# An attention stage whose head groups are put one head after the other, with the projections beside the score units

## The chip, the core and the metric

The kernel runs on one core of a Trainium2 chip. Its time is the device time of that core in microseconds, from launch to end. Five engines work side by side, each with its own queue of instructions, in which everything is done in order: TensorE (PE, matrix products and transposes into PSUM, which has eight banks), VectorE (DVE), ScalarE (ACT), GpSimd (POOL) and SyncE (SP), which here only issues DMAs. They wait for each other by semaphores: a wait stands in front of an instruction and holds up everything behind it in the same queue.

## The reference

Two layers of a streaming encoder, on 1024 prompt frames and on 8 running streams of 16 frames. The first is a gated linear recurrence, the second multi-head latent attention. The change is in the attention of the prompt:

```python
cq = rms_norm(proj[..., :Q_LORA], q_norm_g)
q = einsum('btr,re->bte', cq, w_uq).reshape(bsz, t, B_HEADS, NOPE_DIM + ROPE_DIM)
q_rope = rope(q[..., NOPE_DIM:], pos)
# 16 heads; per head, blocks of 128 queries against all earlier keys (chunks of 64)
s = (q_nope . (c w_uk) + q_rope . kr) * (128 + 64) ** -0.5
p = softmax(where(key_chunk <= q_chunk, s, -1e30))
out = (p @ (c w_uv)) * silu(gate)
```

The queries of the 128 sample rows are only projected here (q_lat, q_rope) and used in the samples' attention, the next stage.

## The kernel before

The stages follow each other: recurrence (to about 550 us), output product and norms of layer one, input product of layer two (to about 1000), attention of the prompt head by head in pairs (to about 1667), attention of the samples (to about 1850), output product. Each fp32 product is made of three passes over a high and a low part: ScalarE rounds a value to the high part, VectorE subtracts for the low one, TensorE runs low*high, high*low, high*high (lines 118 to 120).

Attention works on pairs of heads, `body(pr, first, last)`, eight times (the middle six in a loop). A pair consists of two kinds of work.

*Projections*, in the order of `PROJ` (19 steps): QA0 to QA2 and QB0 to QB2 (queries of head A and B, three groups of 384 rows), R0 to R2 (the part of both heads' queries that is rotated), KA0, KA1, KB0, KB1 (keys), V0 to V3 (values), UT and QL (for the samples' queries). Each writes one bank; ScalarE and VectorE then read it, and `proj_out` says that it is free. The R steps are read by VectorE alone (`rope`, one multiplication of 128 partitions and four of 32), then GpSimd adds two halves, ScalarE rounds (the last group with a copy for the samples ahead of it) and VectorE makes the low part (`rope_low`). The scratch of the rotation lies in `p`, the tile of attention weights, so that the first weights (`exp(0)`) and the last rotation exclude each other.

*Score units*, 16 of them, u = 0 to 15, in the order of `ORDER`: a group is (head, 256 queries), a unit is 128 of its queries, and groups are taken two at a time with their units alternating (`unit`, `place_of`). A unit has between one and eight blocks of keys. Its steps: `scores` (TensorE into bank 0, 1 or both for even u, 2 or 3 or both for odd u; it waits until `exp` two units before has read them), `largest` (VectorE), `exp` (ScalarE), `inverted` (VectorE), the scaling by GpSimd, `turn` (TensorE, transposes through banks 4 to 6, rounded by ScalarE and VectorE in `turned`), and for each group `values` (TensorE, bank 7), `gated` (VectorE, the multiplication by the gate) and the store of the result.

All engines walk the same list, by hand: `scores` runs three units ahead of `turn`. Eleven projections (R0 to V0) come ahead of unit 0 and the next pair's QA0, QA1, QA2 and QB0 beside units 14 to 16. SP loads two gates ahead, stores each group's result, and at the beginning of the last pair issues the samples' first loads (`samples.load_first`).

## Time and profile before

| | us |
|---|---|
| median of 3 runs | 2052.42 (2051.8 to 2053.69) |
| the profiled execution | 2052.9 |
| its span, first to last instruction | 2051.1 |
| TensorE busy | 1936.9 (94%) |
| VectorE, ScalarE, GpSimd busy | 1116.0, 721.4, 467.5 |
| mean granted clock of TensorE | 0.984 |

"Busy" counts the time in which at least one instruction runs on the engine. For matmuls, which overlap, it says how long there was any, and their distance in time (from start to start) says what one costs. A row of the timeline with a bracket gives the idle time ahead of it and the instruction whose end released it. The granted clock is 1.00 at 2.4 GHz and 0.50 at 1.2.

### The profile page before, as it was taken

To read this page: it belongs to the slowest core of one execution; us is meant where nothing else is said; L and a number is where in the kernel's file an instruction comes from. 1 tells how busy PE (TensorE), PEld (TensorE's weight loads), DVE (VectorE), ACT (ScalarE), POOL (GpSimd) and SP (SyncE) were. 2 spreads that over 40 slices of the span, in tenths; PEclk is the share of its full clock that TensorE was granted. 3 is DMA by queue.
4 is the path that set the end of the run, shared out by engine and by line. 5 is a ranking of instruction groups with operands and counts; after the bars stand their busy time and mean duration, and the time that the engine had idled before them with its cause. 6 is when DMAs were issued, how large, how long until landed. Compare 5 with 4: busy or idle time off the path is not lost.

```text
span 2051.1 us, 31461 instructions
## 1 busy us (share of the span) xinstructions
PE 1936.9 (94%) x11755; PEld 1821.6 (89%) x11755; DVE 1116.0 (54%) x1964; ACT 721.4 (35%) x1247; POOL 467.5 (23%) x390
## 2 busy tenths in 40 slices
PE   7999999999869999999999999999899889999997
PEld 6999999999848899999989989888899779988886
DVE  3365545654657612332466676666666666763643
ACT  3333232323221132211254453543534447761100
POOL 0121222212211110000153352544433510000111
PEclk9999999999979999999999999999999989999999
DMA  5121122211164212232211110211111412364421
GB/s 163 42 75 45 41 73 65 64 32 53 35 228 138 88 44 76 76 101 76 85 56 51 42 50 23 65 49 32 55 50 41 128 55 68 94 226 139 139 92 41
DMA packets 190337, 158.78 MB, mean 77 GB/s; under 512 B 36176, under 2 KB 174928, under 8 KB 190000
## 3 DMA queue, kind: packets, MB, share of 16 engines
q1 hardware_dynamic: 184608, 137.31, 22.0%
q10 hardware_dynamic: 5184, 18.88, 2.6%
q0 software_dynamic: 464, 1.48, 0.2%
q8 instruction: 56, 0.92, 0.2%
q14 instruction: 25, 0.20, 0.0%
HBM read 115.78 MB, written 41.84 MB: 77 GB/s over the span
## 4 chain that ended last, share of the span: by engine, by line
PE 46%; issue 11%; DVE 5%; ACT 4%; POOL 3%; SPq 1%; DMA 1%; ACTq 0%; DVEq 0%; POOLq 0%
PE ps L118 14%; PE ps L120 13%; PE ps L119 13%; POOL h_p L1595 3%; PE ps L1699 1%; DVE h_mx L1894 1%; PE ps L1682 1%; PE ps L1681 1%; ACT h_p L1793 1%; DVE s_mx L2448 1%; DMA m_w_raw<-in_w_out_a 1%; SPq L2067 1%; DVE h_pt_l L112 1%; PE ps L2157 0%; ACT h_w_h L107 0%
## 5 line engine op out<-in xcount | busy, mean ns | idle before, releaser
L118 PE MATMUL a_pj<-act_h,a_w_l 128*128 128x384 f32 x768 | 276.8, 360 | 7.5 <-DVE act_l L112 7.5
L1600 POOL TENSOR_SCALAR h_p<-h_p,h_rsum 128x128 f32<-128x128 f32 (+7 forms) x128 | 220.4, 1728 | 220.9 <-DVE h_rsum L1898 220.2
L119 PE MATMUL a_pj<-act_l,a_w_h 128*128 128x384 f32 x768 | 261.2, 340 | 0.0
L120 PE MATMUL a_pj<-act_h,a_w_h 128*128 128x384 f32 x768 | 260.8, 340 | 0.0
L118 PE MATMUL ps<-act_h,m_c_l 128*128 128x384 f32 x480 | 163.7, 341 | 4.1 <-DVE act_l L112 2.4
L120 PE MATMUL ps<-act_h,m_c_h 128*128 128x384 f32 x480 | 163.3, 340 | 0.0
L119 PE MATMUL ps<-act_l,m_c_h 128*128 128x384 f32 x480 | 163.1, 340 | 0.0
L118 PEld LDWEIGHTS a_pj<-act_h,a_w_l 128*128 128x128 f32 x768 | 145.3, 189 | 12.8 <-DVE act_l L112 8.2
L119 PEld LDWEIGHTS a_pj<-act_l,a_w_h 128*128 128x128 f32 x768 | 145.6, 190 | 3.4 <-issue 3.4
L120 PEld LDWEIGHTS a_pj<-act_h,a_w_h 128*128 128x128 f32 x768 | 145.2, 189 | 0.0
L107 ACT ACTIVATE h_pt_h<-ps 128x128 fp32r<-128x128 f32 (+2 forms) x192 | 87.0, 489 | 114.6 <-PE ps L1699 113.5
L1793 ACT ACTIVATE h_p<-ps,h_mx 128x128 f32<-128x128 f32 (+7 forms) x128 | 95.0, 742 | 85.5 <-DVE h_mx L1894 81.1
L118 PE MATMUL ps<-o_w,o_g 128*128 128x512 f32 x288 | 112.1, 389 | 0.0
L119 PE MATMUL ps<-o_w,o_g 128*128 128x512 f32 x288 | 112.0, 389 | 0.0
L120 PE MATMUL ps<-o_w,o_g 128*128 128x512 f32 x288 | 112.0, 389 | 0.0
L112 DVE TENSOR_TENSOR h_pt_l<-ps,h_pt_h 128x128 fp32r<-128x128 f32 (+2 forms) x192 | 100.2, 550 | 19.1 <-ACT h_pt_h L107 18.9
L118 PE MATMUL ps<-h_pt_h,h_v_l 128*128 128x256 f32 x320 | 93.4, 292 | 15.9 <-DVE h_gate L1912 15.9
L1595 POOL TENSOR_TENSOR h_p<-h_p 64x384 f32<-64x384 f32 x48 | 58.4, 1217 | 208.0 <-DVE h_p L1853 206.6
L1894 DVE TENSOR_REDUCE h_mx<-ps 128x1 f32<-128x128 f32 (+7 forms) x128 | 97.0, 758 | 4.4
L118 PE MATMUL ps<-cq_h,h_w_l 128*128 128x384 f32 x288 | 97.7, 339 | 1.4 <-ACT h_pt_l L1811 1.4
L118 PE MATMUL ps<-h_kt_h,h_qn_l 128*128 128x384 f32 (+4 forms) x192 | 75.2, 391 | 23.9 <-ACT h_p L1793 16.4
L120 PE MATMUL ps<-cq_h,h_w_h 128*128 128x384 f32 x288 | 96.4, 335 | 0.0
(325 smaller groups left out, 4978.4 us busy)
## 6 DMA issues: line engine op xcount, KB each, us to landing
a_w_raw<-in_w_in_a SPq DMA_DIRECT2D x32, 512.0 KB, 4.1
m_c_raw<-in_w_in_b SPq DMA_DIRECT2D x20, 512.0 KB, 4.1
scratch_gate<-m_sg SPq DMA_DIRECT2D x16, 576.0 KB, 5.1
h_gate<-scratch_gate SPq DMA_DIRECT2D x64, 128.0 KB, 2.0
scratch_og<-h_gate SPq DMA_DIRECT2D x64, 128.0 KB, 1.7
o_w_raw<-in_w_out_b SPq DMA_DIRECT2D x16, 512.0 KB, 6.9
o_g_raw<-scratch_og SPq DMA_DIRECT2D x24, 256.0 KB, 4.1
a_factors<-in_x SPq DMA_DIRECT2D x9, 512.0 KB, 5.3
```

What stands on the lines that cost most here:

```text
L107: return nc.scalar.activation(high, x, ACT.Identity)
L112: return nc.vector.tensor_tensor(low, x, high.bitcast(F32), ALU.subtract)
L118: nc.tensor.matmul(out, ll, rh, start=first, stop=False)
L119: nc.tensor.matmul(out, lh, rl, start=False, stop=False)
L120: return nc.tensor.matmul(out, lh, rh, start=False, stop=last)
L1595: done = nc.gpsimd.tensor_tensor(rope_sums(tg)[:, e], rope_part(tg, 0)[rows], rope_part(tg, 1)[rows], ALU.add)
L1600: nc.gpsimd.tensor_scalar(weights_of(u), weights_of(u), rsum[:, u % PB], None, ALU.mult).then_inc(S["p_ready"], 1)
L1681: nc.tensor.matmul(out, rq[:, e, q], k.kr_l[:, kc], start=False, stop=False)
L1682: mm = nc.tensor.matmul(out, rq[:, e, q], k.kr_h[:, kc], start=False, stop=True)
L1699: mm = nc.tensor.transpose(bank[:, 4 + i % TB, j * P:j * P + P], p[:, u % PB, key * P:(key + 1) * P], k.ident[:])
L1793: nc.scalar.activation(weights_of(u), scores_of(u), ACT.Exp, bias=mx[:, u % PB], accum_out=rsum[:, u % PB]).then_inc(S["exp_done"], 1)
L1894: nc.vector.tensor_reduce(mx[:, u % PB], scores_of(u), AX.X if n <= BANK else AX.XY, ALU.max, negate=True).then_inc(S["max_done"], 1)
```

## The change

The groups are taken head by head: all four of head A, then all four of head B, a small one (at most four blocks of keys) together with a large one. As the even units are now the small ones, they need only bank 0, and bank 1 is free for one projection at a time. So the second head's projections and the sample step QL stand beside units 0 to 7 (`BESIDE`), the next pair's QA0, QA1, KA0, KA1 and QA2 beside units 9 to 13, and R0, R1, R2 around the last two value products. Ahead of unit 0 only V0 remains, ahead of unit 1 V1, UT, V2 and V3. `exp(0)` waits for the last rotated group. The weights of the next pair are split in units 6 to 8, two pieces each, instead of one piece in each of units 5 to 10. ScalarE does `exp(u + 3)` ahead of `turned(u)` instead of behind it. SP stores the sample queries after group 2 and issues the samples' loads, in the last pair, after group 4; ScalarE and VectorE take the first sample queries in unit 13 instead of 8.

```diff
@@ -1399,7 +1399,7 @@
-ORDER = [(0, 0), (1, 3), (0, 1), (1, 2), (1, 1), (0, 2), (1, 0), (0, 3)]
+ORDER = [(0, 0), (0, 2), (0, 1), (0, 3), (1, 0), (1, 2), (1, 1), (1, 3)]
...
-PROJ = ["QA0", "QA1", "QA2", "QB0", "R0", "R1", "R2", "QB1", "QB2", "UT", "KA0", "KA1", "KB0", "KB1",
-        "V0", "V1", "QL", "V2", "V3"]
-
-READS = ["QA0", "QA1", "QA2", "QB0", "R0", "QB1", "R1", "QB2", "UT", "KA0", "R2", "KA1", "KB0", "KB1",
-         "V0", "V1", "QL", "V2", "V3"]
-PROJ_BANK = [i % 8 for i in range(12)] + [4, 5, 6, 7, 4, 5, 6]
+PROJ = ["QA0", "QA1", "KA0", "KA1", "QA2", "R0", "R1", "R2", "V0", "V1", "UT", "V2", "V3",
+        "KB0", "QB0", "KB1", "QB1", "QB2", "QL"]
 NP = len(PROJ)
+PLACE = {"R1": 0, "R2": 2, "V0": 3, "V1": 4, "V2": 5, "V3": 6}
+FIRST_PLACE = {"QA0": 0, "KA0": 2, "KA1": 3, "QA2": 4, "R0": 5}
 HIGH_COUNT = {s: sum(x[0] != "R" for x in PROJ[:i + 1]) for i, s in enumerate(PROJ)}
...
-EARLY = {14: ["QA0"], 15: ["QA1"], 16: ["QA2", "QB0"]}
-NE = 4
+BESIDE = {0: ("KB0", 0), 1: ("QB0", 0), 2: ("KB1", 0), 3: ("QB1", 0), 5: ("QB2", 0), 7: ("QL", 0),
+          9: ("QA0", 1), 10: ("QA1", 1), 11: ("KA0", 1), 12: ("KA1", 1), 13: ("QA2", 1)}
+NE = 5
+
+
+def place(s, first):
+
+    return FIRST_PLACE[s] if first and s in FIRST_PLACE else PLACE.get(s, 1)
+
 PIECES = [2 * QD] * 4 + [2 * GQ] * 2
...
-            sp.wait_ge(S["proj_out"], pr * NP + NP)
-            sp.dma_start(d["scratch_ql"][bass.ds(pr, 1)].rearrange("o p t -> p (o t)"), flat(qlat[:])).then_inc(S["ql_stored"], 16)
-            sp.dma_start(d["scratch_qr"][bass.ds(pr, 1)].rearrange("o p t -> p (o t)"), flat(qr[0:RD])).then_inc(S["qr_stored"], 16)
-            if last:
-
-                sp.wait_ge(S["ql_stored"], 16 * PAIRS)
-                sp.wait_ge(S["qr_stored"], 16 * PAIRS)
-                k.samples.load_first(sp)
-            else:
+            if not last:
                 load_w(sp, pr + 1, False)
             for g in range(NG):
...
                     load_gate(pr, g + 2, False)
+                if g == 2:
+                    sp.wait_ge(S["proj_out"], pr * NP + NP)
+                    sp.dma_start(d["scratch_ql"][bass.ds(pr, 1)].rearrange("o p t -> p (o t)"), flat(qlat[:])).then_inc(S["ql_stored"], 16)
+                    sp.dma_start(d["scratch_qr"][bass.ds(pr, 1)].rearrange("o p t -> p (o t)"), flat(qr[0:RD])).then_inc(S["qr_stored"], 16)
+                if g == 4 and last:
+
+                    sp.wait_ge(S["ql_stored"], 16 * PAIRS)
+                    sp.wait_ge(S["qr_stored"], 16 * PAIRS)
+                    k.samples.load_first(sp)
         pairs(sp, body)
...
                 nc.gpsimd.tensor_scalar(weights_of(u), weights_of(u), rsum[:, u % PB], None, ALU.mult).then_inc(S["p_ready"], 1)
-                if last and u == 2:
+                if last and u == 10:
                     pool.wait_ge(S["proj_out"], PAIRS * NP)
                     k.samples.zero_first(pool)
+            if not last:
+                rope_adds(pr + 1)
         pairs(pool, body)
...
         def proj(pr, s, first):
-            i, b = STEP[s], PROJ_BANK[STEP[s]]
-            earlier = [j for j in range(i) if PROJ_BANK[j] == b]
+            i, b = STEP[s], place(s, first)
+            earlier = [j for j in range(i) if place(PROJ[j], first) == b]
             if s == "QA0":
                 pe.wait_ge(S["wl_ready"], pr * WPARTS + 4)
-            if s == "UT":
+            if s == "KA0":
                 pe.wait_ge(S["wl_ready"], pr * WPARTS + WPARTS)
             if earlier:
                 pe.wait_ge(S["proj_out"], pr * NP + earlier[-1] + 1)
             elif first:
                 k.bank_free(pe, b)
+            elif b == 1:
+                pe.wait_ge(S["proj_out"], pr * NP)
+            elif b < 4:
+
+                pe.wait_ge(S["exp_done"], pr * UNITS - 1 + b // 2)
             else:
-
-                if b < 4:
-                    pe.wait_ge(S["exp_done"], pr * UNITS - 1 + b // 2)
...
-
-                pe.wait_ge(S["proj_out"], pr * NP + STEP[("KA1", "KB1")[u]] + 1)
-                pe.wait_ge(S["rq_out"], pr * 3 + (1, 3)[u])
+                pe.wait_ge(S["proj_out"], pr * NP + STEP[("R1", "V0")[u]] + 1)
             else:
                 pe.wait_ge(S["exp_done"], pr * UNITS + u - 1)
+            if u in (0, 1, 5):
+
+                pe.wait_ge(S["rq_out"], pr * 3 + (1, 2, 3)[min(u, 2)])
+            if u in (8, 9, 13):
+
...
             proj(0, s, True)
         pe.wait_ge(S["zeroed"], 4)
         def body(pr, first, last):
-            for s in PROJ[NE:]:
-                if s in ("V1", "QL"):
-                    scores(pr, ("V1", "QL").index(s))
+            proj(pr, "V0", first)
+            scores(pr, 0)
+            for s in ("V1", "UT", "V2", "V3"):
                 proj(pr, s, first)
+            scores(pr, 1)
             scores(pr, 2)
             for u in range(UNITS):
+                if u in BESIDE and not (last and BESIDE[u][1]):
+                    s, n = BESIDE[u]
+                    proj(pr + n, s, first and not n)
                 if u + 3 < UNITS:
                     scores(pr, u + 3)
                 if u >= 4 and u % 4 < 2:
-                    values(pr, u // 4 * 2 - 2 + u % 2)
-                if u in EARLY and not last:
-                    for s in EARLY[u]:
-                        proj(pr + 1, s, False)
+                    values(pr, u // 4 * 2 - 2 + u % 2, first)
+                if u == UNITS - 1 and not last:
+                    proj(pr + 1, "R0", False)
                 turn(pr, u)
-            values(pr, NG - 2)
+            values(pr, NG - 2, first)
             if not last:
-                for s in EARLY[UNITS]:
-                    proj(pr + 1, s, False)
+                proj(pr + 1, "R1", False)
             else:
                 k.samples.turn_first(pe)
-            values(pr, NG - 1)
+            values(pr, NG - 1, first)
+            if not last:
+                proj(pr + 1, "R2", False)
...
         def exp(pr, u):
             act.wait_ge(S["max_done"], pr * UNITS + u + 1)
+            if u == 0:
+
+                act.wait_ge(S["rq_out"], pr * 3 + 3)
             if u >= PB:
...
         def body(pr, first, last):
-            for s in READS[NE:]:
-                if s == "V1":
-                    exp(pr, 0)
-                if s == "QL":
-                    exp(pr, 1)
+            proj(pr, "V0", first)
+            exp(pr, 0)
+            for s in ("V1", "UT", "V2", "V3"):
                 proj(pr, s, first)
+            exp(pr, 1)
             exp(pr, 2)
             for u in range(UNITS):
-                if u in EARLY and not last:
-                    for s in EARLY[u]:
-                        proj(pr + 1, s, False)
-                turned(pr, u)
+                if u in BESIDE and not (last and BESIDE[u][1]):
+                    s, n = BESIDE[u]
+                    proj(pr + n, s, first and not n)
                 if u + 3 < UNITS:
                     exp(pr, u + 3)
-                if 5 <= u < 5 + WPARTS and not last:
-                    split_high(act, pr + 1, u - 5)
-                if last and u == 8:
+                turned(pr, u)
+                if 6 <= u < 9 and not last:
+                    split_high(act, pr + 1, 2 * (u - 6))
+                    split_high(act, pr + 1, 2 * (u - 6) + 1)
+                if last and u == 13:
                     k.samples.first_queries_high(act)
             if not last:
-                for s in EARLY[UNITS]:
+                for s in ("R0", "R1", "R2"):
                     proj(pr + 1, s, False)
             else:
                 k.samples.first_keys_high(act)
...
         dve.wait_ge(S["table_loaded"], 32)
+        rope(0, 0, True)
+        rope(0, 1, True)
+
+        def ropes_end(pr, first):
+            rope_low(pr, 0)
+
+            dve.wait_ge(S["rq_out"], pr * 3 + 1)
+            rope(pr, 2, first)
+            rope_low(pr, 1)
+            rope_low(pr, 2)
+
+        ropes_end(0, True)
         def body(pr, first, last):
-            rope(pr, 0)
-            rope(pr, 1)
-            rope_low(pr, 0)
-
-            dve.wait_ge(S["rq_out"], pr * 3 + 1)
-            rope(pr, 2)
-            for s in READS[NE + 1:]:
-                if s[0] == "R":
-                    rope_low(pr, int(s[1]))
-                    continue
-                if s == "V1":
-                    largest(pr, 0)
-                if s == "QL":
-                    inverted(pr, 0)
-                    largest(pr, 1)
-                proj(pr, s)
+            proj(pr, "V0", first)
+            largest(pr, 0)
+            for s in ("V1", "UT", "V2", "V3"):
+                proj(pr, s, first)
+            inverted(pr, 0)
+            largest(pr, 1)
             inverted(pr, 1)
             largest(pr, 2)
             for u in range(UNITS):
                 if u + 2 < UNITS:
                     inverted(pr, u + 2)
+                if u in BESIDE and not (last and BESIDE[u][1]):
+                    s, n = BESIDE[u]
+                    proj(pr + n, s, first and not n)
                 if u + 3 < UNITS:
                     largest(pr, u + 3)
                 if u >= 4 and u % 4 < 2:
                     gated(pr, u // 4 * 2 - 2 + u % 2)
-                if u in EARLY and not last:
-                    for s in EARLY[u]:
-                        proj(pr + 1, s)
                 turned(pr, u)
-                if 5 <= u < 5 + WPARTS and not last:
-                    split_low(dve, pr + 1, u - 5)
-                if last and u == 8:
+                if 6 <= u < 9 and not last:
+                    split_low(dve, pr + 1, 2 * (u - 6))
+                    split_low(dve, pr + 1, 2 * (u - 6) + 1)
+                if last and u == 13:
                     k.samples.first_queries_low(dve)
             gated(pr, NG - 2)
             if not last:
-                for s in EARLY[UNITS]:
-                    proj(pr + 1, s)
+                rope(pr + 1, 0, False)
             else:
                 k.samples.first_keys_low(dve)
             gated(pr, NG - 1)
+            if not last:
+                rope(pr + 1, 1, False)
+                ropes_end(pr + 1, False)
```

VectorE, from one pair to the next. Before, in the new pair; h_p with h_cos and h_sin is `rope`, h_rq is `rope_low`, h_qn_l, h_kt_l and h_v_l are low parts of the queries of one head, keys and values, MEMSET and h_mx are `largest`:

```order
L1851 TENSOR_TENSOR h_p<-ps,h_cos 128x384
L1853 TENSOR_TENSOR h_p<-ps,h_sin 32x384 x4
...
L1866 SCALAR_TENSOR_TENSOR h_qn_l<-ps,h_qn_h 128x384
L1866 SCALAR_TENSOR_TENSOR h_rq<-h_p,h_rq 64x2x384
...
L1866 SCALAR_TENSOR_TENSOR h_qn_l<-ps,h_qn_h 128x384
...
L112 TENSOR_TENSOR h_kt_l<-ps,h_kt_h 128x512
L1866 SCALAR_TENSOR_TENSOR h_rq<-h_p,h_rq 64x2x384
...
L112 TENSOR_TENSOR h_kt_l<-ps,h_kt_h 128x512
...
L112 TENSOR_TENSOR h_v_l<-ps,h_v_h 128x512
...
L1890 MEMSET ps 64x64
L1894 TENSOR_REDUCE h_mx<-ps 128x1
```

After, from the last gate multiplication of a pair (h_gate) on:

```order
L1937 TENSOR_TENSOR h_gate<-ps,h_gate 128x256
L1876 TENSOR_TENSOR h_p<-ps,h_cos 128x384
L1878 TENSOR_TENSOR h_p<-ps,h_sin 32x384 x4
L1891 SCALAR_TENSOR_TENSOR h_rq<-h_p,h_rq 64x2x384
L1876 TENSOR_TENSOR h_p<-ps,h_cos 128x384
L1878 TENSOR_TENSOR h_p<-ps,h_sin 32x384 x4
L1891 SCALAR_TENSOR_TENSOR h_rq<-h_p,h_rq 64x2x384 x2
...
L112 TENSOR_TENSOR h_v_l<-ps,h_v_h 128x512
...
L1915 MEMSET ps 64x64
L1919 TENSOR_REDUCE h_mx<-ps 128x1
```

Between the last `rope` and the first `largest` stood two query parts, four key parts and one value part; now only the value part stands there, and the last gate multiplication of the pair before stands ahead of rope(1).

SP in the last pair. Before (scratch_og is the store of a group, h_gate the load of a gate, s_ql, s_qr, s_kr, s_c and in_cache_ckv the samples' loads):

```order
L1569 DMA scratch_ql<-h_qlat 128x512
L1570 DMA scratch_qr<-h_qr 64x256
L2071 DMA s_ql_raw<-scratch_ql 128x8x512
L2072 DMA s_qr_raw<-scratch_qr 64x8x256
L2063 DMA h_w_raw<-in_cache_ckv 128x8x256
...
L2067 DMA s_kr_raw<-out_krope_sample 16x64
L1581 DMA scratch_og<-h_gate 128x256
L1562 DMA h_gate<-scratch_gate 128x256
L1581 DMA scratch_og<-h_gate 128x256
L1562 DMA h_gate<-scratch_gate 128x256
```

After:

```order
L1578 DMA scratch_og<-h_gate 128x256
L1567 DMA h_gate<-scratch_gate 128x256
L2103 DMA s_ql_raw<-scratch_ql 128x8x512
L2104 DMA s_qr_raw<-scratch_qr 64x8x256
L2095 DMA h_w_raw<-in_cache_ckv 128x8x256
...
L2099 DMA s_kr_raw<-out_krope_sample 16x64
L1578 DMA scratch_og<-h_gate 128x256
L1567 DMA h_gate<-scratch_gate 128x256
L1578 DMA scratch_og<-h_gate 128x256 x2
```

The samples' loads moved behind the stores of five groups and the load of the seventh gate; the eighth gate's load stands behind them.

## Rows read from the trace of the kernel before

**Rows 1.** The page, part 1: busy us, share of the span, instructions.

```profile
PE 1936.9 (94%) x11755; PEld 1821.6 (89%) x11755; DVE 1116.0 (54%) x1964; ACT 721.4 (35%) x1247; POOL 467.5 (23%) x390
```

**Rows 2.** One head pair: us, busy (instructions), clock, DMA share, GB/s.

```profile
1191.00:1273.20 82.20, 77.09 (x504) 1.00 0.15 45
```

**Rows 3.** Waits of TensorE in 1000 to 1600: total us, times, longest us.

```profile
PE ps L118 <- ACT h_p L1793: 15.1, 21, 1.2
...
PE ps L118 <- DVE h_gate L1912: 9.9, 14, 1.0
...
PE ps L118 <- DVE h_kt_l L112: 6.8, 7, 1.0
...
PE ps L1699 <- POOL h_p L1600: 2.8, 7, 0.4
...
PE ps L1699 <- DVE h_pt_l L112: 1.3, 6, 0.2
```

**Rows 4.** Timeline, TensorE, start of a pair: start, us, [idle before <-releaser].

```profile
1287.60 0.41 PE L118 MATMUL ps<-h_kt_h,h_qn_l 128*128 128x320 f32 x1 [0.38 <-ACT h_p L1793]
```

**Rows 5.** Timeline, TensorE: first and thirteenth matmul of a row, 384 and 256 columns.

```profile
1257.05 0.33 PE L118 MATMUL ps<-cq_h,h_w_l 128*128 128x384 f32 x1
...
1259.13 0.33 PE L118 MATMUL ps<-cq_h,h_w_l 128*128 128x384 f32 x1
...
1192.32 0.28 PE L118 MATMUL ps<-h_w_h,ct_l 128*128 128x256 f32 x1
...
1193.76 0.37 PE L118 MATMUL ps<-h_kt_h,h_qn_l 128*128 128x448 f32 x1
```

**Rows 6.** Timeline, VectorE, start of a pair: rope(1), rope_low(0), the last rope_low.

```profile
1260.31 0.56 DVE L1851 TENSOR_TENSOR h_p<-ps,h_cos 128x384 f32<-128x384 f32 x1 [0.23 <-DVE h_p L1853]
...
1263.29 1.75 DVE L1866 SCALAR_TENSOR_TENSOR h_rq<-h_p,h_rq 64x768 fp32r<-64x768 f32 x1 [0.15 <-DVE h_p L1853]
...
1272.07 0.95 DVE L1866 SCALAR_TENSOR_TENSOR h_rq<-h_p,h_rq 64x768 fp32r<-64x768 f32 x1 [0.98 <-ACT h_rq L1767]
```

**Rows 7.** Timeline, GpSimd: the rotation's last two adds.

```profile
1268.07 2.71 POOL L1595 TENSOR_TENSOR h_p<-h_p 64x384 f32<-64x384 f32 x2 [2.16 <-DVE h_p L1853]
```

**Rows 8.** Timeline, ScalarE: copy and rounding of the last group.

```profile
1270.88 0.41 ACT L1766 COPY h_qr<-h_p 64x256 f32<-64x256 f32 x1 [2.60 <-POOL h_p L1595]
...
1271.19 0.84 ACT L1767 ACTIVATE h_rq<-h_p 64x768 fp32r<-64x768 f32 x1
```

**Rows 9.** Timeline: V's two roundings, largest and exp of five key blocks.

```profile
1274.85 0.68 DVE L112 TENSOR_TENSOR h_v_l<-ps,h_v_h 128x512 fp32r<-128x512 f32 x1
...
1276.37 0.59 ACT L107 ACTIVATE h_v_h<-ps 128x512 fp32r<-128x512 f32 x1
...
1289.73 0.82 DVE L1894 TENSOR_REDUCE h_mx<-ps 128x1 f32<-128x640 f32 x1
...
1619.21 0.80 ACT L1793 ACTIVATE h_p<-ps,h_mx 128x640 f32<-128x640 f32 x1 [0.62 <-DVE h_mx L1894]
```

**Rows 10.** Timeline, SP queue, last pair: first load, last key load, next store.

```profile
1614.37 0.39 SPq L2071 DMA_DIRECT2D s_ql_raw<-scratch_ql  x1
...
1627.38 2.28 SPq L2067 DMA_DIRECT2D s_kr_raw<-out_krope_sample  x1
...
1635.81 0.42 SPq L1581 DMA_DIRECT2D scratch_og<-h_gate  x1
```

**Rows 11.** Timeline, TensorE, last pair: values(3).

```profile
1641.10 0.55 PE L118 MATMUL ps<-h_pt_h,h_v_l 128*128 128x256 f32 x1 [5.55 <-DVE h_gate L1912]
```

**Rows 12.** Stretches with slow clock: us, busy (instructions), granted clock, DMA share, GB/s.

```profile
720.00:725.00 5.00, 4.75 (x19) 0.67 0.07 14
...
1642.00:1650.00 8.00, 8.00 (x45) 0.70 0.25 79
```

**Rows 13.** DMA issues: KB each, median us to landing.

```profile
s_qr_raw<-scratch_qr SPq DMA_DIRECT2D x1, 512.0 KB, 12.2
```

**Rows 14.** Timeline, TensorE, in the stage before attention.

```profile
720.25 0.44 PE L118 MATMUL ps<-act_h,m_c_l 128*128 128x384 f32 x1 [2.37 <-DVE act_l L112]
```

42 lines of the change are left out of this document (23 added, 19 removed).

## The prediction

> **What bounds the kernel now.** I read the page first: TensorE is busy 1936.9 of 2051.1 us [rows 1], so time goes either into its matmuls, which the change leaves as they are in kind and number, or into its waits. Then a table by stretches. One head pair lasts 82.2 us, of which TensorE is busy 77.1 at full clock [rows 2]; the reader is to see that 5.1 us a pair, 41 us over eight pairs, is all that any new order of the attention stage can win. Then the waits, summed over the first seven pairs [rows 3]. The largest are 15.1 us for the exponential (21 times, three a pair), 9.9 us for the gate multiply (14 times), 6.8 us for the second head's keys (once a pair, at the first score unit), and 2.8 and 1.3 us for scaled or turned weights just behind it. One of a pair's three waits for the exponential, 0.38 us, lies in the first units as well [rows 4]. So some 2.0 us (1.0 + 0.4 + 0.38 + 0.2) belong to the start of a pair, and 3.1 us to its middle, where a unit has nothing beside it.
>
> **What the change moves.** The names R0 to R2, V0 to V3, UT are the projection steps; s0, s1, ... the score units, exp, largest and turn what follows each of them. Before, behind a pair's last value product TensorE had R0, R1, R2, QB1, QB2, UT, KA0, KA1, KB0, KB1 and V0 to do before s0. They hid the rotation of the queries, a chain through four engines. After, R0 and R1 come a little earlier (before the last transposes and before the last values), but behind the last value product only R2, V0, s0, V1, UT, V2 and V3 are left before s1. Everything else lies beside units.
>
> *Start of a pair.* I call the end of the last value product 0. Twelve matmuls of 384 columns take 2.08 us and twelve of 256 take 1.44 [rows 5]. By that TensorE is through with R2 at 2.1 and with V0 at 3.55. On VectorE the last gate multiply ends at about 0.5, and only then come rope(1), rope_low(0), rope(2), rope_low(1) and rope_low(2). The same chain stands in the trace: rope(1) starts at 1260.31, rope_low(0) at 1263.29 and takes 1.75, and the last rope_low starts at 1272.07 and takes 0.95 [rows 6]. In between lie GpSimd's two adds for the last group, 2.71 us [rows 7], and ScalarE's copy and rounding, 1270.88 to 1272.03 [rows 8]. From start to end that is 12.7 us. Nothing of this is shorter in the new order, since its links wait for each other and not for TensorE; R2 is there in time, at 2.1. So rope_low(0) ends at 0.5 + 2.98 + 1.75 = 5.2 and the last rope_low at 13.1 to 13.2. V0's low part stands behind it in VectorE's queue, and takes 0.68 [rows 9]: 13.8.
> - s0 waits for rope_low(0) and for rope(1), whose bank it takes: 5.35 against 3.55, a wait of 1.8.
> - s0 (0.6), V1, UT (0.45), V2, V3 (three of 1.44) end at 10.75. s1 takes the banks of R2 and V0, so it waits for V0's low part: 13.85, a wait of 3.1.
> - s1 (ten matmuls of 320 columns), s2 and KB0 take 1.5 + 0.6 + 1.4 and end at 17.4. s3 waits for exp(1). Behind V0's low part come largest(0) 0.45, exp(0) 0.55, four roundings on ScalarE of some 0.5 (V1, UT, V2, V3; a row says 0.59, with starts closer than that), V3's low part 0.7, and largest(1) and exp(1) at 0.82 + 0.25 and 0.80 + 0.19 [rows 9]: 13.8 + 6.0 = 19.8. A wait of 2.3 to 2.4.
> - QB0 takes KB0's bank: KB0's two roundings follow exp(2), and TensorE waits about 0.7.
>
> Together 7.9 us against 2.0. There are eight such starts (the first has the same chain behind QA2, with R0 to R2 in a row): 5.9 x 8 = **+47**. Below, if the links overlap better, I put 3 a start, above 7.
>
> *Middle of a pair.* From unit 3 each unit has 1.4 to 2.1 us of projection beside it, and small and large units alternate. The waits for the exponential and for the gate are 0.5 to 1.2 us each; a projection in front covers each of them. Units 4, 6 and 8 have none (or QL's 1.05 in 7), but the widths there are mixed and I find no late exponential. What goes is 3.1 a pair in the first seven; the last pair has no next projections in its second half and gains nearly nothing: 3.1 x 7 = **-22**. It can't be more; at least zero.
>
> *A new wait for weights.* The six pieces of the next pair's weights are split in units 6 to 8, two a unit, and QA0 now needs four of them in unit 9. VectorE has some 9.2 us to do in units 6 to 8: three maxima 2.6, turned weights 2.1, six pieces 3.6 (some 0.6 each, near V's low part in size), a gate and reciprocals 0.9. TensorE has 8.1: three score units 3.9, QL and values(2) 2.5, turns 1.7. VectorE enters unit 6 about as late as it leaves it, with 1.4 us of chain behind TensorE's last score, so the fourth piece is out 1.7 us after TensorE asks for QA0, in the 7 pairs that have one, **+12**, between 0 and 20.
>
> *The last pair.* Before, the samples' first loads are issued at its start (1614.37), and the SP queue is free for the next store only at 1635.81: 21.4 us, for the queue is full [rows 10]. The gate of group 2 waits behind them, and TensorE stands 5.55 us [rows 11]; afterwards its clock is granted at 0.70 in 1642 to 1650 [rows 12], a mean between 2.4 GHz and 1.2, that is 2.4 us of work lost there. After, the same loads come behind the gate load for group 6, when gated(4) is done. I count from the end of s15: gated(4) at 2.0, its store landed and the gate load issued at 4.5. So the loads start at X = 4.5. The rotary queries land 12.2 us after issue [rows 13], which is at X + 12.6 = 17.1; ScalarE and VectorE wait for them in unit 13, in front of the transposed weights of units 14 and 15. The two split the queries in 1.0 and 1.2 us, values(6) starts at 20.2 instead of about 7.5, and the first keys' last load, issued 13.0 behind X [rows 10], lands at about 22.8. The sample transposes (3.3) and values(7) (2.9), in part at half clock, end at about 31. In the trace of before the last value product ends 13.8 behind s15. That is 17 more, less the 5.55 and the slow clock behind it (7.4 together, taken down by the usual wait of 0.9 and a little more at half clock): **+10**, between -7 (the loads are no hindrance) and +19.
>
> **Sum.** 47 - 22 + 12 + 10 = +47. The profiled execution took 2052.9 us around its span of 2051.1; the median of the three runs, 2052.42, is 0.5 below it. 2052.9 + 47 = 2100.
>
> **Rivals.**
> - *The clock falls at each start of a pair.* Where TensorE had waited 2.37 us, the next 5 us were granted 0.67 [rows 12, 14]: two thirds of them at 1.2 GHz, 1.65 us lost. Now a wait of 3.1 and one of 2.3 stand 3.5 us apart. What is slow between them is hidden by the second wait, what comes behind it is not: 1.65 x 8 = +13, so 2113, at most double. Against it: waits up to 1.2 left the clock at 1.00 [rows 2]. The Trainium skill (TensorE: Matmul & The Clock Gate, Part 1, HAM oscillation) says that gaps in the supply of matmuls put the array back to half rate and that it comes back only with sustained work; by that page this change, which gathers idle time in one place instead of spreading it, would pay the clock too, which is this rival and no part of my sum.
> - *The start is covered.* TensorE has 6.8 us of work between R2 and s1. If V0's low part were out at 8.9 instead of 13.8, s1 would not wait, and from 7 on neither s3. Then the work would hide the chain as eight projections did before, each start would stay at 2.0, and only the middle would count: 2052.9 - 22 + 10 = 2041, faster. For it: three of the V steps and UT are free of the chain. Against it: the 12.7 us of rows 6, which include no wait for TensorE.
> - *The last pair costs nothing*, since the queue takes the loads faster beside less other traffic: 47 - 22 + 12 - 7 = +30, 2083.
>
> **Chances.** Forecast 0.50, clock 0.20, last pair free 0.15, start covered 0.12, a mixture near no change 0.03. Range: the likeliest case's own is 2080 to 2120 (starts at 4.5 to 7 us, weights 0 to 20, end -7 to +19, not all at one side); toward the cheap starts it goes to 3 x 8 - 22 + 6 + 5 = +13, 2066, and with the clock to 2130. A measurement of this kernel can tell 0.2% (4 us) from no change. Faster 0.12, within 0.2% 0.04, slower 0.84.
>
> **What would show it.** In the profile after, seven times in the steady stage: TensorE waits of 1 to 3 us at the first, second and fourth score unit, released by VectorE (the rotated queries' low part, V's low part) and ScalarE (exponential); no waits of the gate multiply at TensorE; a wait for the split weights at QA0; a pair of about 87 us instead of 82.2. In the last pair, a wait of ScalarE of some 10 us at the samples' queries with TensorE standing behind it, and none at the gate of group 2. Wrong, if the second score unit waits under 1 us, or if the pair's period is below 82.

## The result, and the profile after

| | before | after |
|---|---|---|
| median of 4 runs, us | 2052.11 (2050.2 to 2053.69) | 2112.32 (2109.76 to 2113.41) |
| ratio, 95% interval | | 1.0292 [1.0274, 1.031] |
| span of the profiled execution | 2051.1 | 2108.0 |
| mean granted clock | 0.984 | 0.970 |

The kernel is 60 us slower. The page of after, part 1, beside [rows 1]: TensorE's share is smaller, and yet it is busy 18 us longer with the same 11755 instructions.

```profile
PE 1954.9 (93%) x11755; PEld 1841.2 (87%) x11755; DVE 1120.1 (53%) x1964; ACT 717.7 (34%) x1247; POOL 467.2 (22%) x390
```

TensorE's waits of after from 1000 to 1640 us (us in total, times, longest), against [rows 3]. The waits for the gate are gone, as are nearly all of those for the exponential. In their place stand V's low part, the split weights and the rotated queries, each once a pair, and one single wait of 11.3 us.

```profile
PE ps L118 <- DVE h_v_l L112: 18.8, 6, 3.2
PE ps L118 <- DVE h_w_l L112: 15.7, 7, 2.3
PE ps L118 <- DVE h_rq L1891: 11.4, 7, 1.7
PE ps L118 <- ACT h_pt_l L1836: 11.3, 1, 11.3
PE ps L118 <- DVE h_kt_l L112: 6.5, 12, 0.6
PE ps L118 <- ACT h_p L1818: 3.2, 4, 1.9
```

The waits of one steady pair, from the timeline of after (start, duration, line, idle time ahead and its releaser). They are those of s0, s1, s3 and QB0, against the 2.0 us before a pair's first units in [rows 3, 4], and at the end that of QA0:

```profile
1195.09 0.39 PE L118 MATMUL ps<-h_kt_h,h_qn_l 128*128 128x256 f32 x1 [1.62 <-DVE h_rq L1891]
1203.86 0.41 PE L118 MATMUL ps<-h_kt_h,h_qn_l 128*128 128x320 f32 x1 [3.17 <-DVE h_v_l L112]
1209.54 0.44 PE L118 MATMUL ps<-h_kt_h,h_qn_l 128*128 128x384 f32 x1 [0.44 <-ACT h_p L1818]
1212.13 0.45 PE L118 MATMUL ps<-cq_h,h_w_l 128*128 128x384 f32 x1 [0.45 <-DVE h_kt_l L112]
1242.24 0.44 PE L118 MATMUL ps<-cq_h,h_w_l 128*128 128x384 f32 x1 [2.26 <-DVE h_w_l L112]
```

The windows of after (us, busy of each engine, clock, DMA share, GB/s): a whole pair, then 4 us behind the wait of an s1, then 4 us around the wait of a QA0. The pair is 6 us longer than in [rows 2], 2.6 of them busy time, and in it the clock is low just behind the two longest waits.

```profile
1278.00:1366.20 88.20, 79.67 (x505) 74.93 (x504) 54.97 (x118) 36.32 (x84) 34.71 (x23) 0.96 0.14 42
1293.00:1297.00 4.00, 4.00 (x18) 3.51 (x16) 2.98 (x6) 2.09 (x7) 0.60 (x1) 0.60 0.00 1
1330.00:1334.00 4.00, 3.42 (x13) 3.43 (x14) 2.84 (x8) 2.19 (x5) 0.93 (x1) 0.66 0.10 33
```

The clock does not fall each time. In the fifth of the eight pairs (1366.7 to 1455.0 us) it stays at 1.00 behind the same wait of 3.17 us ahead of s1. There s3 waits 1.86 us instead of 0.44, and the pair is as long as its neighbours. In the second and the sixth pair it stays at 1.00 behind the same wait ahead of QA0, and these two pairs are 1.6 to 1.7 us shorter. The wait of s3 in the fifth pair with the window behind its s1, and the wait of QA0 in the sixth with the window behind it:

```profile
1386.25 0.44 PE L118 MATMUL ps<-h_kt_h,h_qn_l 128*128 128x384 f32 x1 [1.86 <-ACT h_p L1818]
1381.00:1385.00 4.00, 3.39 (x20) 2.72 (x19) 2.71 (x6) 2.40 (x6) 0.49 (x1) 1.00 0.02 7
1507.23 0.43 PE L118 MATMUL ps<-cq_h,h_w_l 128*128 128x384 f32 x1 [2.27 <-DVE h_w_l L112]
1508.00:1512.00 4.00, 4.00 (x30) 4.00 (x29) 2.84 (x9) 2.58 (x6) 0.70 (x2) 1.00 0.18 59
```

So in this kernel a slow clock behind s1 costs nothing, since s3 waits for ScalarE's exponential in any case, and one behind QA0 costs its full length. Why it falls in one pair and not in another, no run shows.

Where the 60 us are, from the ends of each pair's last value product. Before, pairs follow each other in 82.24 us. After, in 86.6, 88.4, 88.3, 88.3, 86.8 and 88.4: the six pairs in the middle cost 33.4 more. 4.9 us of projections moved from each pair into the one before it. With these counted to the pair that they belong to, the first pair costs 11.5 more and the last 15.8: 60.7 together. In the profiled execution the work ahead of the attention happened to be 3.7 us shorter, which makes the spans differ by 56.9. That part isn't touched by the change: in fourteen profiled kernels the first query projection starts anywhere from 994.2 to 1000.5 us, so below I compare pairs and not spans.

### The profile page after: what moved, and what is told of

Same layout as the page of the kernel before. It is cut to its first block, busy times and chain, and to the rows that moved or that the text cites. A ratio compares the mean times of both kernels' runs of the same rounds, so it can differ in the third digit from the quotient of the medians.

```text
span 2108.0 us, 31531 instructions
## 1 busy us (share of the span) xinstructions
PE 1954.9 (93%) x11755; PEld 1841.2 (87%) x11755; DVE 1120.1 (53%) x1964; ACT 717.7 (34%) x1247; POOL 467.2 (22%) x390
## 4 chain that ended last, share of the span: by engine, by line
PE 46%; issue 9%; DVE 8%; ACT 4%; POOL 3%; DMA 1%; ACTq 0%; SPq 0%; DVEq 0%; POOLq 0%
PE ps L118 14%; PE ps L119 14%; PE ps L120 14%; POOL h_p L1601 2%; DVE h_mx L1919 2%; PE ps L1714 1%; ACT h_pt_h L107 1%; DVE h_pt_l L112 1%; POOL h_p L1610 1%; ACT h_p L1818 1%; PE ps L1697 1%; PE ps L1696 1%; DMA s_qr_raw<-scratch_qr 1%; DVE s_mx L2480 1%; DMA m_w_raw<-in_w_out_a 1%
## 5 line engine op out<-in xcount | busy, mean ns | idle before, releaser
L118 PE MATMUL ps<-cq_h,h_w_l 128*128 128x384 f32 x288 | 103.6, 360 | 18.5 <-DVE h_w_l L112 15.7
L118 PE MATMUL ps<-h_kt_h,h_qn_l 128*128 128x256 f32 (+2 forms) x192 | 72.8, 379 | 37.4 <-DVE h_v_l L112 21.8
L119 PE MATMUL ps<-cq_l,h_w_h 128*128 128x384 f32 x288 | 99.3, 345 | 0.0
```

The lines of the kernel that those rows point to most:

```text
L118: nc.tensor.matmul(out, ll, rh, start=first, stop=False)
L119: nc.tensor.matmul(out, lh, rl, start=False, stop=False)
```

## The experiments

Unless said otherwise an experiment is the changed kernel with one edit. Ratios are to the kernel before, beside it on the same chip; after stands at 1.0292.

**Order of groups alone.** The kernel before, with one line changed.

```diff
-ORDER = [(0, 0), (1, 3), (0, 1), (1, 2), (1, 1), (0, 2), (1, 0), (0, 3)]
+ORDER = [(0, 0), (0, 2), (0, 1), (0, 3), (1, 0), (1, 2), (1, 1), (1, 3)]
```

> The kernel before with one thing of the change alone: the groups head by head, small with large, in place of the mixed order; the projections stay where they were. It asks what the order of groups does by itself. Theory (the waits in the middle of a pair come from units that have no projection beside them, and the start is covered by eight projections): a pair stays within 1 us of 82.2, the middle waits between 2 and 5 us, total within 0.5% of 2052. Rival (a good part of the loss comes from the new order, since the second unit has five blocks instead of seven and units are otherwise in balance): the pair grows by 3 us or more, or shrinks by 2 or more if the better balance is what wins the middle.

Measured 2059.2, ratio 1.0036 [1.0027, 1.0046]. A pair takes 83.4 us, 1.2 more than before. The order of the groups by itself is thus a small part of the 60 us; the rest comes with the other edits, the places of the projections, of the weights' pieces and of the samples' loads.

**The four zero blocks.** In the first pair TensorE stands 11.26 us ahead of V0:

```profile
1021.56 0.58 PE L118 MATMUL ps<-h_w_h,ct_l 128*128 128x256 f32 x1 [11.26 <-ACT h_pt_l L1836]
```

ScalarE's rows there show why. The four small blocks (L1836) stand in its queue behind the rounding of R2, and so behind the whole rotation:

```profile
1019.56 0.40 ACT L1788 COPY h_qr<-h_p 64x256 f32<-64x256 f32 x1 [3.90 <-POOL h_p L1601]
1019.88 0.84 ACT L1789 ACTIVATE h_rq<-h_p 64x768 fp32r<-64x768 f32 x1
1020.62 0.49 ACT L1836 ACTIVATE h_pt_h<-ident 128x128 fp32r<-128x128 f32 x2
1021.02 0.49 ACT L1836 ACTIVATE h_pt_l<-ident 128x128 fp32r<-128x128 f32 x2
```

```diff
-        for s in PROJ[:NE] + ["R0", "R1", "R2"]:
+        for s in PROJ[:NE]:
             proj(0, s, True)
         for x in (pt_h[0], pt_h[1], pt_l[0], pt_l[1]):
             nc.scalar.activation(x[:, 0, 0:P], k.ident[:], ACT.Identity, scale=0.0)...
+        for s in ("R0", "R1", "R2"):
+            proj(0, s, True)
```

> The changed kernel, but in the first pair ScalarE writes the four zero blocks (128 columns of the turned weights) ahead of R0, R1, R2 and not behind them. TensorE waits for these zeros before V0 of the first pair; in the changed kernel that wait was 11.26 us and ended with the zeros. Theory (the zeros stand in ScalarE's queue behind the rotation of the third group, so that V0, s0, V1, UT, V2 and V3 cannot lie beside the chain): the wait goes, and in its place come the waits of any other pair, 1.6 us at s0 and 3.1 us at s1; the 6.8 us of work between them move under the chain, and the granted clock stays at 1.00 in 1012 to 1028. Gain 6 to 9 us, 2112 becomes 2104. Rival (the chain of the first pair takes this long by itself and bounds whatever stands before it): no gain over 2 us, the wait is found again at s0 or s1 at its full size.

Measured 2109.04, 1.0274 [1.0256, 1.0292]. The wait is gone, and the trace has in its place waits like those of every other start (1.62 and 3.17 there):

```profile
1019.71 0.35 PE L118 MATMUL ps<-h_kt_h,h_qn_l 128*128 128x256 f32 x1 [2.36 <-DVE h_rq L1893]
1028.15 0.41 PE L118 MATMUL ps<-h_kt_h,h_qn_l 128*128 128x320 f32 x1 [2.88 <-DVE h_v_l L112]
```

The first pair is 6.3 us shorter. The ratio shows 4 us, and the intervals overlap, so the size rests on the trace.

**Weights one unit earlier.**

```diff
-                if 6 <= u < 9 and not last:
-                    split_high(act, pr + 1, 2 * (u - 6))
+                if 5 <= u < 8 and not last:
+                    split_high(act, pr + 1, 2 * (u - 5))
...
```

(and the same for the other piece and for the low parts on VectorE)

> The changed kernel, but the next pair's six weight pieces are split in units 5, 6 and 7 instead of 6, 7 and 8, two a unit as before. In the changed kernel TensorE waits 2.26 us for the fourth piece at QA0, seven times (15.7 us), and the 8 us behind it were granted 0.70 and 0.88 in part. Theory (VectorE and ScalarE reach the pieces too late for unit 9): the wait goes in every pair, 2.3 us plus up to 1.7 us of slow clock each, 7 times: gain 14 to 25 us, a pair 84.5 to 86 us instead of 88.4. Rival 1 (VectorE's backlog in units 5 to 8 bounds and only moves): TensorE waits as long elsewhere in units 7 to 10, gain under 5 us. Rival 2 (the pieces wait for QB2 at unit 5 and hold up the queue): slower.

Measured 2103.14, 1.0247 [1.023, 1.0264]: 9 us gained, not 14 to 25. QA0 no longer waits, but the fourth value product now does, 1.4 us for the gate, since the pieces stand ahead of that multiplication in VectorE's queue. The window of a pair tells the clock's share: its busy time fell by 1.3 us, and the clock around QA0 is 1.00.

```profile
1192.40:1278.80 86.40, 78.37 (x505) 73.69 (x505) 54.92 (x118) 36.23 (x84) 34.75 (x23) 0.98 0.15 43
1328.00:1332.00 4.00, 4.00 (x29) 4.00 (x28) 2.85 (x8) 2.58 (x6) 1.89 (x1) 1.00 0.00 0
```

So the wait of 2.26 had cost 3.6 with the slow clock behind it, and 1.7 came back at the gate and at a score unit. All six middle pairs take 86.3 to 86.5 us now. In two of them the clock stays at 1.00 behind s1 and s3 waits 1.87 us: no shorter.

**V3 computed three times.** This fills TensorE's idle time ahead of s1 with the same product again.

```diff
-                for j in range(2):
+                for j in [0, 1] * (3 if s == "V3" else 1):
```

> The changed kernel, but TensorE computes V3 three times over (24 more matmuls of 256 columns, 2.9 us, overwriting the same bank with the same values) just ahead of s1, where it waits 3.1 us for V0's low part. Nothing depends on the extra work. It asks what the slow clock behind that wait (0.60 in the 4 us from s1 on) costs. Theory A (the slow clock is hidden, because s3 must wait for exp(1) in any case: the wait at s3 is only 0.44 us because s1, s2 and KB0 ran slowly): the granted clock stays 1.00 there, the wait at s3 grows from 0.44 to 1.5 to 2.3 us, and the time changes by less than 4 us. Theory B (the clock costs 1.65 us at each start of a pair, 8 times): 8 to 14 us faster in spite of more work. Rival C (V3 comes later by the extra work and its roundings delay largest(1) and exp(1)): slower by 2 to 3 us a pair, 16 to 24 us.

Measured 2120.41, 1.0327 [1.0304, 1.0351], whose interval just touches that of after. The wait at s1 shrinks to 0.28, and that at s3 grows from 0.44 to 1.89:

```profile
1300.20 0.41 PE L118 MATMUL ps<-h_kt_h,h_qn_l 128*128 128x320 f32 x1 [0.28 <-DVE h_v_l L112]
1305.88 0.44 PE L118 MATMUL ps<-h_kt_h,h_qn_l 128*128 128x384 f32 x1 [1.89 <-ACT h_p L1818]
```

s3 starts 19.6 us behind the start of the pair in both kernels, so exp(1) did not come later by the added work. At full clock s2 and KB0 are done 1.45 us earlier, and TensorE waits that long for exp(1) instead. In two of the six middle pairs that wait has a low clock behind it. The two windows are of such a pair, behind s1 and behind s3, the second where after had full clock:

```profile
1300.00:1304.00 4.00, 3.79 (x21) 3.17 (x21) 2.58 (x8) 2.41 (x6) 0.00 (x0) 1.00 0.14 48
1306.00:1310.00 4.00, 4.00 (x15) 3.90 (x16) 2.10 (x7) 1.05 (x3) 2.78 (x2) 0.57 0.00 0
```

In after the stretch from 1298 us on, behind its s3, has full clock. Four of the six middle pairs last 88.2 to 88.4 us, as most of after's do: 2.9 us of products went into the idle time and the full clock behind s1 brought nothing. The two pairs with a slow stretch behind s3 last 89.2. And here the clock fell behind QA0 in all six, where after has two pairs without that. These two things make the 5.0 us by which the six are longer; 1.9 more are in the first pair, where TensorE has no wait ahead of s1 that the products could fill. The rest of the 8 us of the medians is not placed.

**The samples' loads in two parts**, the first behind group 2 instead of 4.

```diff
+                    if last:
+                        k.samples.load_first(sp)    # g == 2: queries and sequence 0
                 if g == 4 and last:
-                    k.samples.load_first(sp)
+                    k.samples.load_second(sp)       # sequence 1
```

> The changed kernel, but in the last pair the samples' first loads are issued in two parts: queries and the first stream's keys behind the stores of group 2 (unit 8), the second stream's keys behind group 4; GpSimd zeroes their padding in unit 7 instead of 10. Theory (ScalarE's wait for the sample queries in unit 13, 9.85 us, holds the turned weights of units 14 and 15 and so TensorE, 11.40 us): that wait goes to nothing, as the queries have some 12 us more; TensorE's clock does not fall in 1706 to 1718; gain 11 to 16 us. A small price: the gate of group 5 may come late by up to 3 us. Rival (the queue, full for 15 us, moves the stall to a gate, as in the kernel before at group 2, 5.5 us): TensorE waits for a gate multiply of group 4 or 5 by 5 us or more, and the gain is under 7 us.

Measured 2106.07, 1.0272 [1.0251, 1.0293], whose interval overlaps that of after. By the traces the last pair is 5.4 us shorter, not 11 to 16. The wait of 11.40 us turned into one of 7.25. VectorE's row shows what took its place: the gate of group 5 lands 9.4 us late, as its load stands in the queue of SP behind 16 us of issues.

```profile
1706.26 0.42 DVE L1938 TENSOR_TENSOR h_gate<-ps,h_gate 128x256 f32<-128x256 f32 x1 [9.36 <-DMA h_gate<-scratch_gate]
```

**Rotation earlier.** R0, R1 and R2 each one step earlier on TensorE (ahead of the turns of units 14 and 15 and of the last value product), rope(0) and rope(1) ahead of `turned` of these units. GpSimd's adds of the rotation now wait for its own last scaling.

```diff
+                if u >= UNITS - 2 and not last:
+                    rope(pr + 1, u - UNITS + 2, False)
                 turned(pr, u)
...
             gated(pr, NG - 2)
-            if not last:
-                rope(pr + 1, 0, False)
...
             gated(pr, NG - 1)
             if not last:
-                rope(pr + 1, 1, False)
```

> The changed kernel, but the next pair's R0 stands ahead of the transposes of unit 14, R1 ahead of those of unit 15 and R2 between the last two value products; VectorE rotates group 0 ahead of the turned weights of unit 14 and group 1 ahead of those of unit 15, so rope_low(0) follows the last-but-one gate multiply and no rotation but the third waits for the last one. (GpSimd waits for its own last scaling before the adds.) Theory (the start of a pair is bound by the chain from rope(1), begun at 0.5 us behind the last value product, to V0's low part at 13.8): the last rope_low ends some 5 to 6 us earlier against the last value product; the wait at s0 (1.62) goes, that at s1 (3.17) goes down to 0 to 1, the one at s3 comes up to 1 to 2.3 because its chain from V0's low part is unchanged; a new wait of 0 to 1 at the last values. Gain 2.5 to 4 us a pair, 7 pairs: 17 to 28 us. Rival (VectorE has no room at the end of the pair, turned weights of unit 15 come late by the 2.8 us of a rotation): TensorE waits 2 us or more at the last value product and the gain is under 7 us.

Measured 2115.36, 1.0304 [1.0285, 1.0323]: no gain, and my reason for it was wrong. s0 no longer waits, s1 waits 3.17 us as ever, and 1.2 us came new at the last two value products. VectorE's timeline shows it:

```profile
1284.04 0.42 DVE L1937 TENSOR_TENSOR h_gate<-ps,h_gate 128x256 f32<-128x256 f32 x1 [3.23 <-PE ps L120]
1284.49 0.95 DVE L1891 SCALAR_TENSOR_TENSOR h_rq<-h_p,h_rq 64x768 fp32r<-64x768 f32 x1
1285.57 0.56 DVE L1876 TENSOR_TENSOR h_p<-ps,h_cos 128x384 f32<-128x384 f32 x1
...
1292.47 0.95 DVE L1891 SCALAR_TENSOR_TENSOR h_rq<-h_p,h_rq 64x768 fp32r<-64x768 f32 x1 [2.17 <-ACT h_rq L1789]
1293.45 0.69 DVE L112 TENSOR_TENSOR h_v_l<-ps,h_v_h 128x512 fp32r<-128x512 f32 x1
```

R2's product was done before the last value product began, but its rotation stands behind the last gate multiplication, and that waits 3.2 us for the end of that product. Rotating R0 and R1 earlier can't help as long as the last group's rotation starts there.

**Rotation of R2 ahead of the last gate**, on top of that. rope(1) moves with it, from ahead of the turned weights of unit 15 to behind the last gate but one.

```diff
             gated(pr, NG - 2)
+            if not last:
+                rope(pr + 1, 1, False)
+                rope_low(pr + 1, 0)
+                dve.wait_ge(S["rq_out"], (pr + 1) * 3 + 1)
+                rope(pr + 1, 2, False)
...
             gated(pr, NG - 1)
```

> e_rope with another order on VectorE at the end of a pair: last products' gate of group 6, then R1's rotation, the low part of R0, R2's rotation, and only then the gate of group 7, which waits for the end of the last value product (in e_rope the rotation of R2 stood behind that gate, from 1284.04 to 1285.57, though its product was done some 4 us before). Theory A (that place in VectorE's queue kept e_rope from gaining): the last low part of the rotation comes about 4 us earlier, the waits of 1.6 us ahead of s0 and 3.2 us ahead of s1 are both gone, and with them some 1.4 us of half clock behind them; pair about 82.5 instead of 88.4, less what e_rope added (0.5 + 0.7): about 2068, between 2060 and 2080. Theory B (V0's roundings in ScalarE's queue and exp(0) hold back s2 and s3 in any case): the waits move to s2 and s3 as in e_best (1.1 + 2.0 per pair): 2090 to 2100.

Measured 2096.89, 1.0219 [1.0202, 1.0236], 18 us under the kernel without this edit. About 3 of them are the clock's, which stays up behind QA0 in three of the six middle pairs instead of one. The time is in the range of the second theory, not of the first (2060 to 2080), but the wait that is left is at s1 and not at s2 and s3. The place of the rotation in VectorE's queue is thus what held the former up. But s1 still waits 2.28 us for V0's low part, which stands behind the last low part of the rotation, and GpSimd and ScalarE still need 3.9 us between R2's rotation and that:

```profile
1286.07 0.95 DVE L1891 SCALAR_TENSOR_TENSOR h_rq<-h_p,h_rq 64x768 fp32r<-64x768 f32 x1 [2.17 <-ACT h_rq L1789]
1287.05 0.69 DVE L112 TENSOR_TENSOR h_v_l<-ps,h_v_h 128x512 fp32r<-128x512 f32 x1
```

**V0 and the first maximum ahead of the last rotated group**, on the kernel with the zero blocks moved (1.0274).

```diff
             rope_low(pr, 1)
+            proj(pr, "V0", first)
+            largest(pr, 0)
             rope_low(pr, 2)
```

(on VectorE; on ScalarE V0's high part stands ahead of the rounding of R2 and V1's ahead of exp(0))

> e_zero with one edit: V0's roundings (ScalarE's high part, VectorE's low part) and the largest value of unit 0 stand ahead of the last rotated group's rounding and low part, V1's high part ahead of exp(0). Theory A (s1's wait of 3.17 us in each pair is V0's low part standing behind the last low part of the rotation in VectorE's queue): V0's low part is made some 2 to 4 us earlier and the wait ahead of s1 is gone; a part comes back at s2 and s3, since exp(0) still waits for the last rotated group (as e_best shows, 1.1 + 2.0): net 1 to 3 us a pair, and s0's 1.6 stays: 2109 - 8 x 2 = 2093, between 2085 and 2102. Theory B (the rotation's chain itself, from R2's products behind the last value product over GpSimd, is what every unit waits for): nothing gained beyond 3 us, the 3.2 us appear again at s2 and s3: 2105 to 2112.

Measured 2100.98, 1.0238 [1.0223, 1.0254]: some 7 us. s1 doesn't wait any more, but 3.1 us come back at s2 and s3, of what s1 and s3 had waited, 3.6:

```profile
1284.63 0.38 PE L118 MATMUL ps<-h_kt_h,h_qn_l 128*128 128x256 f32 x1 [1.09 <-ACT h_p L1818]
1288.89 0.44 PE L118 MATMUL ps<-h_kt_h,h_qn_l 128*128 128x384 f32 x1 [2.01 <-ACT h_p L1818]
```

s2 waits for exp(0), which may not start before the rotation has left its scratch. And s3 waits for exp(1): between s1 and s3 TensorE has only s2 and KB0, some 2 us, and the way over largest(1) and exp(1) takes 2.0 more. That comes with the new places of the projections. Before, QL, V2 and V3 stood there.

**All together, in four steps.** The first has all the corrections above except the rotation of R2 ahead of the last gate.

> All corrections together: zeros ahead of the rotation, weights in units 5 to 7, the samples' loads in two parts from group 2 on, the earlier rotation, and V0's roundings and the first maximum ahead of the last rotated group on ScalarE and VectorE (V1's high part ahead of exp(0)). Theory (the change wins 3.1 us a pair in the middle, and loses it at the start, at the weights and at both ends of the stage): a pair takes 79 to 81 us, less than the 82.2 of the kernel before; waits of 0.5 to 1.5 us at s3 remain; total 2018 to 2045, faster than both. Rival (TensorE's waits are conserved by VectorE, which is 68% busy and in order): a pair stays over 83 us, total over 2060.

2079.66, 1.0136 [1.0118, 1.0155], far above the 2018 to 2045 of the theory; the rival came true. 33 us are won back of 60, and s2 and s3 wait 1.1 and 2.0 in each pair, as in the last experiment. The second step adds R2's rotation ahead of the last gate, the weights spread over units 3 to 7, and the samples' loads spread over groups 2 to 6.

> e_best with three things more: VectorE's order of e_rope2; the next pair's weights rounded one or two pieces at a time, those of keys and values first, in units 3 to 7; and the samples' loads of the last pair spread, one or two behind each group from 2 to 6, so that no gate waits behind them. From e_best's waits: s2 and s3 1.1 + 2.0 gone in 8 pairs (25 us), the gate at the third value product 1.43 to about 0.5 (7 us), the wait for the last gate 0.72 (4 us), the turn of unit 15 in the last pair 5.84 (up to 5 us): 2080 - 41 = 2039, between 2030 and 2052. If it falls below 2052 the new order of the work beats the one before once its chains are in order. Theory B: the waits come back elsewhere (the rotation's last low part is still the last to end, exp(0) waits for it): 2060 to 2072, not under before.

2071.75, 1.0105 [1.0087, 1.0123], above the range of the first theory and at the top of the second. s3's 2.01 us stayed, as it isn't the rotation that it waits for, and the last piece of weights came 1.7 us late for QA0. The third puts V3 between s1 and s2, all pieces in units 3 to 6, and the large loads behind groups 3 and 5.

```diff
-            for s in ("V1", "UT", "V2", "V3"):
+            for s in ("V1", "UT", "V2"):
                 proj(pr, s, first)
             scores(pr, 1)
+            proj(pr, "V3", first)
             scores(pr, 2)
```

> e_best2 with three places mended that its trace shows: V3 stands between s1 and s2 instead of ahead of s1 (TensorE, ScalarE behind exp(1), VectorE behind the largest of unit 1), so that the way from s1 over the largest value and exp(1) to s3, 2.01 us of idle time in each pair, is covered by V3's products, and exp(0) to s2 (0.25 to 1.2 us) too: 8 x 2.5 = 20 us; the last two pieces of the weights in unit 6, as 1.7 us ahead of QA0 were waited for: 7 x 1.7 = 12, less what comes back at the gates (up to 1.0 each); the samples' large loads behind groups 3 and 5 only, since the last trace has the gate of group 5 land 8.6 us late behind them: up to 3.8. Theory A: 2071.8 - 20 - 8 - 3 = 2041, between 2032 and 2050, under before. Theory B (s1 now waits for what V3 gave the rotation's low part and V0 time to do, 1.7 us in each pair): 2041 + 14 = 2055, no better than before.

2062.58, 1.0054 [1.0041, 1.0068], above both theories (2041 and 2055). Its pair takes 82.1 to 82.4 us and is as good as before's. A pair of this kernel:

```profile
1178.20:1260.40 82.20, 76.90 (x505) 72.15 (x505) 54.24 (x119) 36.22 (x84) 34.71 (x23) 1.00 0.15 45
```

Of the 6.1 us a pair nothing is left, and 77 us of busy time at full clock stand against 79.7. It waits 5 us a pair in other places (s3 1.3, QB0 1.5, five below 0.7). The remaining 10 us are in the first pair (about 3) and in the last (about 9, with the projections again counted to their own pair); the work ahead of the attention happened to be 4.4 us shorter in this trace.

The fourth step moves QB0, KB1 and QB1 one unit later, loads the first cache rows at the start of the last pair and the queries behind group 3.

> e_best3 with two edits, each with its own place in the trace. (1) QB0, KB1 and QB1 stand one unit later, beside units 2 to 4 (1.53 us of wait for KB0's low part ahead of QB0 in each pair): 8 x 1.5 = 12 us less, unless the waits come back at QB1 or at the ninth unit's scores. (2) In the last pair the cache rows of the first sample sequence are loaded at its start, where no gate is stored for 30 us, the sample queries behind group 3 and the small rows behind group 4; ScalarE and VectorE take the queries in unit 15: of 2.95 + 1.13 + 4.95 us of waits at the end of e_best3 some 5 go. Theory A: 2062.6 - 12 - 5 = 2046, between 2038 and 2054; level with or under before. Theory B (the idle 1.5 us is only moved to the next wait for a largest value and its exponential, as every wait in this run of units so far): 2053 to 2062.

2063.61, 1.0055 [1.0041, 1.0069]: no gain in sum. The first edit did as its second theory had it. The 1.53 us ahead of QB0 went, and 0.31 at the next score unit, 1.13 ahead of KB1 and 0.4 ahead of QB1 came, so that a pair takes 83.0 us, 0.6 more:

```profile
1112.80 0.44 PE L118 MATMUL ps<-h_kt_h,h_qn_l 128*128 128x384 f32 x1 [0.31 <-ACT h_p L1835]
1120.06 0.50 PE L118 MATMUL ps<-ct_h,h_w_l 128*128 128x512 f32 x1 [1.13 <-DVE h_qn_l L1910]
```

The second edit did what was expected of it: the last pair takes 80.6 us instead of 85.3. Without the first edit the kernel might be 4 us faster (an estimate from the 0.6 us in each of six pairs); that was not run. No version beats the kernel before.

## Why the prediction was right, and where not

It said 2100 (2066 to 2130) and slower; the kernel takes 2112.3. By its own terms, us in a steady pair of 88.3 (four of the six are such), and in brackets the one of them whose clock stays up behind s1:

| term | predicted | measured |
|---|---|---|
| start, s0 / s1 / s3 / QB0 | 1.8 / 3.1 / 2.3 / 0.7, less 2.0: +5.9 | 1.62 / 3.17 / 0.44 / 0.45, less 2.0: +3.7 (s3 1.86: +5.1) |
| middle | -3.1 | -2.5 (0.61 waits for KA0's low part) |
| wait for weights | +1.7 | +2.3 |
| clock | 0 | +2.6 (+1.3) |
| sum | +4.5 | +6.1 |

- **The start.** The chain came out as worked out, link by link: the last rope_low starts at 1290.42, 12.3 us behind the last value product (TensorE goes on with R2 at 1278.16), where I had 12.2, and s0 and s1 are within 0.2 us. The experiments with V0 and with R2's rotation show that it is this chain, in VectorE's queue, that s1 waits for. What came out otherwise is the wait at s3: I had all of s1, s2 and KB0 at full clock. In most pairs they ran at about half for a while, which took 1.4 of its 1.86 us. In the pair where they did not, the four waits are 7.1 us where I had 7.9.
- **The clock** was a rival of 0.20 with 1.65 us at each start. Shown: it falls in five of the six middle pairs behind s1's wait of 3.17 us (to 0.60 in the one shown). That costs nothing there, as the fifth pair and V3 computed three times show: s3's wait is shorter by as much. It costs in full where the rival didn't look, around QA0 (0.66), with nothing late behind it: taking that wait away brought 1.3 us of busy time back, and the two pairs in which the clock stays up there are 1.6 to 1.7 us shorter. That the rival's 2113 is close to the result is chance: its 1.65 us at each start are not paid, and the 1.3 to 1.7 us at QA0 are not in it.
- **The weights.** Right in mechanism, 2.26 instead of 1.7, and I left out the slow clock behind them: 3.6 together (weights one unit earlier). The 1.7 does not follow from the figures beside it either: 9.2 + 1.4 - 8.1 less the last two pieces' 1.2 is 1.3.
- **The middle.** The gate and exponential waits went as I had it. The new 0.61 us is KA1's for KA0's low part, since both use bank 1. I had not counted what follows from one bank for all the projections.
- **The first pair** costs 11.5 and not 4.5. The step that failed is "the first has the same chain behind QA2". I followed VectorE's queue there and not ScalarE's, where the zero blocks stand behind R2. Worth 6.3 us in the trace: with them moved the first pair costs 5.2.
- **The last pair** costs 15.8; the sum had 5.9 + 10 = 15.9. So close a match is partly luck, since the waits of its start are 3.6 more than 2.0 and not 5.9. The chain at the end is the one foreseen: ScalarE waits 9.85 us for the sample queries, and the value product starts at 1714.27, 16.3 us behind the first of the loads (1698.00), where I had 15.7.

```profile
1711.17 0.72 ACT L2303 ACTIVATE s_q_h<-s_ql_raw 128x256 fp32r<-128x256 f32 x2 [9.85 <-DMA s_qr_raw<-scratch_qr]
```

In all: the six steady pairs (33.4 instead of 27) and the first one (11.5 instead of 4.5) make the 13 us between forecast and result. "Start covered" fell, as s1 does wait over 3 us. The last pair's cost is for the most part avoidable. With the loads in two parts it is still 10.4 us, as the gates go through the same queue. With the loads spread over more groups, and the start mended too (second and fourth combined kernel), the whole last pair costs 4 us more than before's.

## What to carry to other kernels

Work that TensorE can do while a chain through other engines runs is worth most right behind the start of the chain. Spread here beside units that wait 0.5 us each, it saves 2.5 us a pair and leaves 3.2 us bare in one place. When a wait is taken away, look for the next instruction in the same queue that waits for something else: here V0's low part, R2's rotation and the zero blocks each stood behind a wait that had nothing to do with them. A slow clock counts only where nothing later in the chain waits anyway. And judge a reordering only when its queues are in order: the new order of groups alone costs 7 of the 60 us, and with its chains mended the steady pair is level with before, but not ahead.
